# Attention of layer 1: row sums turned on the matrix engine and applied to the output, one operation for bias and maximum, turned blocks copied by two engines

## The reference

```
sc = (q . k) / sqrt(64) - slope * distance          # -inf for keys not chosen or in the future
pr = softmax(sc)                                     # exp(sc - max) / sum
o  = pr @ v
```

## Time and profile before

| | us |
|---|---|
| median of 3 runs | 1532.46 |
| lowest and highest | 1531.11, 1533.18 |
| the profiled execution | 1534.15 |
| its span, first to last instruction | 1532.3 |
| PE busy in the span | 1454.4 (95%) |
| DVE busy | 675.2 (44%) |
| ACT busy | 605.5 (40%) |
| POOL busy | 568.9 (37%) |

### The profile page before, as it was taken

The page is one execution under the profiler, slowest core; times in us unless marked ns, Lnnn a source line. Parts: engine busy times, 40 slices in busy tenths (PEclk is TensorE's granted clock), DMA queues, the critical chain, the costliest instruction groups (busy, mean ns, idle before and its releaser), DMA issues.

```text
span 1532.3 us, 24569 instructions
## 1 busy us (share of the span) xinstructions
PE 1454.4 (95%) x10321; PEld 1155.2 (75%) x10321; DVE 675.2 (44%) x1059; ACT 605.5 (40%) x872; POOL 568.9 (37%) x265
## 2 busy tenths in 40 slices
PE   7999989888899999999999999978999999999998
PEld 5787668888768888888887787744468888888886
DVE  4666656777563413223144207868823314132231
ACT  5525553434454313232233335557834313132231
POOL 3543331001033434434344242417944443434341
PEclk9999999999999999999999999998999999999999
DMA  4332200000113232322224121210012323232231
GB/s 141 97 96 69 79 5 3 3 3 3 58 58 107 83 110 83 110 82 97 95 82 106 60 83 55 83 55 1 1 56 84 109 88 105 83 102 89 89 102 55
DMA packets 128392, 110.00 MB, mean 72 GB/s; under 512 B 10678, under 2 KB 126512, under 8 KB 128304
## 3 DMA queue, kind: packets, MB, share of 16 engines
q1 hardware_dynamic: 127712, 107.64, 22.8%
q10 hardware_dynamic: 592, 1.07, 0.2%
HBM read 106.60 MB, written 2.10 MB: 71 GB/s over the span
## 4 chain that ended last, share of the span: by engine, by line
PE 78%; DVE 10%; ACT 5%; POOL 3%; issue 2%; DMA 1%; DVEq 0%; ACTq 0%; SPq 0%; POOLq 0%
PE ps L515 21%; PE ps L510 21%; PE ps L511 21%; PE ps L647 5%; DVE lower L1897 2%; DVE lower L1893 1%; POOL lower L2110 1%; PE ps L662 1%; ACT lower L1395 1%; PE ps L547 1%; POOL pw_lo L2001 1%; PE ps L655 1%; PE ps L624 1%; PE ps L751 1%; DVE lower L1676 1%
## 5 line engine op out<-in xcount | busy, mean ns | idle before, releaser
L2078 POOL TENSOR_TENSOR w_lo<-lower,w_hi 128x2048 fp32r<-128x2048 f32 x84 | 387.9, 4618 | 627.1 <-ACT w_hi L1051 627.1
L510 PE MATMUL ps<-h_hi,w_hi 128*128 128x512 f32 x792 | 314.5, 397 | 2.4 <-ACT h_hi L1056 1.7
L511 PE MATMUL ps<-h_hi,w_lo 128*128 128x512 f32 x792 | 313.1, 395 | 0.0
L1051 ACT ACTIVATE w_hi<-lower 128x2048 fp32r<-128x2048 f32 x84 | 160.2, 1907 | 242.8 <-PE ps L515 242.8
L515 PE MATMUL ps<-h_lo,w_hi 128*128 128x512 f32 x792 | 201.8, 396 | 0.4
L511 PE MATMUL ps<-a_hi,w_lo 128*128 128x512 f32 x480 | 189.1, 394 | 0.0
L510 PE MATMUL ps<-a_hi,w_hi 128*128 128x512 f32 x480 | 189.1, 394 | 0.0
L510 PEld LDWEIGHTS ps<-h_hi,w_hi 128*128 128x128 f32 x792 | 149.1, 188 | 41.6 <-issue 5.4
L515 PEld LDWEIGHTS ps<-h_lo,w_hi 128*128 128x128 f32 x792 | 148.7, 188 | 37.6 <-DVE h_lo L1599 2.0
L511 PEld LDWEIGHTS ps<-h_hi,w_lo 128*128 128x128 f32 x792 | 149.3, 188 | 35.3 <-issue 0.5
L1842 DVE TENSOR_TENSOR lower<-lower,ps 128x512 f32<-128x512 f32 x64 | 44.0, 688 | 268.7 <-PE ps L515 268.7
(11 more groups left out here) (358 smaller groups left out, 1991.0 us busy)
## 6 DMA issues: line engine op xcount, KB each, us to landing
lower<-in_mlp_w_dram SPq DMA_DIRECT2D x64, 1024.0 KB, 5.4
lower<-in_ev_w_in_dram SPq DMA_DIRECT2D x30, 512.0 KB, 3.8
lower<-in_od_w_in_dram SPq DMA_DIRECT2D x10, 1024.0 KB, 5.2
lower<-in_ev_w_out_dram SPq DMA_DIRECT2D x4, 1024.0 KB, 5.2
lower<-in_od_w_out_dram SPq DMA_DIRECT2D x4, 1024.0 KB, 5.1
out_dram<-lower SPq DMA_DIRECT2D x4, 512.0 KB, 3.2
lower<-in_od_w_in_dram SPq DMA_DIRECT2D x6, 256.0 KB, 3.8
upper<-in_x_dram SPq DMA_DIRECT2D x1, 1024.0 KB, 7.5
```

Source lines behind the costliest of these rows:

```text
L510: pe.matmul(o, wh, xh, start=(i_ == 0), stop=False)
L511: pe.matmul(o, wl, xh, start=False, stop=False)
L1051: act.activation(WH[:, u % 2, :, 0:w], RAW[:, u % 2, :, 0:w], ACT.Copy).then_inc(hi_ready, 1)
L2078: pool.tensor_tensor(WL[:, u % 2, :, 0:w], RAW[:, u % 2, :, 0:w], as_f32(WH[:, u % 2, :, 0:w]), ALU.subtract)\
```

## The change

The buffer isn't multiplied by the reciprocals any more. POOL spreads the two reciprocals of each row over 2 x 64 columns (`wide_sums`), PE turns this 128x128 block (`row_sums`) into bank 6, ACT copies the bank once for each block b (`sums_out`), and DVE multiplies the product of the values by it (`scaled_values`), while it moves it from bank 7 to SBUF. From there ACT makes the high part and POOL (instead of DVE) the rest.

Bias and row maximum are one operation (`tensor_tensor_reduce`), which needs the same factor for both inputs; so the queries are divided by the slope in advance (`QSCALE`, `QW`, four operations of 512 in place of one of 2048), the sign is turned, and the minimum is taken in place of the maximum.

The turned blocks of head 0 are still copied by ACT, and those of head 1 by DVE. PE's and DVE's loops get a new order, as the diff shows.

```diff
-        SLOPE = small(16)
-        QW = small(2)
+        QSCALE, QW = small(2 * PAIRS), small(2 * PAIRS)
...
+        PV = [L1[:, 20, :], flat(o_att + (2 * TT + 2) * W, W)]
+        RB = DIST
+        RSW = [flat(o_score + 4 * W + i * P, P) for i in range(3)]
...
+        at_pt = [sem("at_pt_act"), sem("at_pt_dve")]
+        VALUES, SUMS = 7, 6
+        def slope(b, p):
+            return float(np.float32(2.0) ** np.float32(-0.5 * (2 * (b % PAIRS * 2 + p) + b // PAIRS + 1)))
...
             def turned(n):
                 i, rows, wdt = rows_of(n)
                 for p in range(2):
-                    pe.wait_ge(at_n, 2 * n + p + 1)
+                    pe.wait_ge(at_p, 2 * n + p + 1)
                     if n >= 1:
-                        pe.wait_ge(at_pt, 2 * (n - 1) + p + 1)
+                        pe.wait_ge(at_pt[p], n)
...
             def values(b):
-                pe.wait_ge(at_pt, 2 * TT * (b + 1))
-                if b >= 2:
-                    pe.wait_ge(mix_lo, KT + b - 1)
+                if b >= 1:
+                    pe.wait_ge(at_pv, b)
+                for p in range(2):
+                    pe.wait_ge(at_pt[p], TT * (b + 1))
...
+            def row_sums(n):
+                i, rows, _ = rows_of(n)
+                pe.wait_ge(at_rw, n + 1)
+                if i == 0 and n >= TT:
+                    pe.wait_ge(at_rb, n // TT)
+                mm = pe.transpose(bank[SUMS][:, rows], RSW[n % 3], IDENT)
+                mm.then_inc(at_rs, 1)
 
             scores(0)
             scores(1)
...
                     scores(n + 2)
                 if n >= LAG:
                     turned(n - LAG)
+                    if n > LAG:
+                        row_sums(n - LAG - 1)
                     if n - LAG >= TT and (n - LAG) % TT == 0:
                         values((n - LAG) // TT - 1)
+            row_sums(STEPS - 1)
             values(2 * PAIRS - 1)
-            pe.wait_ge(mix_lo, KT + 2 * PAIRS - 1)
+            pe.wait_ge(at_rb, 2 * PAIRS)
...
-                    act.wait_ge(at_mx, 2 * n + p + 1)
+                    act.wait_ge(at_z, 2 * n + p + 1)
                     z = ZB[n % NZ][:, p, 0:wdt]
-                    act.activation(z, z, ACT.Exp, bias=NMX[:, col:col + 1],
+                    act.activation(z, z, ACT.Exp, bias=NMX[:, col:col + 1], scale=-1.0,
...
+            def sums_out(b):
+                act.wait_ge(at_rs, TT * (b + 1))
+                if b >= 1:
+                    act.wait_ge(at_pv, b)
+                act.activation(RB, bank[SUMS][:, :], ACT.Copy).then_inc(at_rb, 1)
...
             for n in range(STEPS + LAG):
                 if n < STEPS:
                     probs(n)
                 m = n - LAG
                 if m >= 0:
-                    if m >= TT + 1 and m % TT == 1:
+                    if m > TT and m % TT == 1:
+                        sums_out(m // TT - 1)
+                    if m > TT and m % TT == 3:
                         mixed(m // TT - 1)
                     out_turned(m)
...
-                dve.scalar_tensor_tensor(out=wide(L1[:, lo:lo + 4, :]), in0=wide(L1[:, lo:lo + 4, :]),
-                                         scalar=wgt, in1=wide(rs), op0=mul, op1=mul).then_inc(n_used, 1)
+                for c in range(4):
+                    x = L1[:, lo + c, :]
+                    ins = dve.scalar_tensor_tensor(out=x, in0=x, scalar=QW[:, lo + c:lo + c + 1] if lo < 8 else pc2(MKN),
+                                                   in1=rs[:, c, :], op0=mul, op1=mul)
+                ins.then_inc(n_used, 1)
...
+                dve.tensor_tensor_reduce(out=ZB[n % NZ][:, p, 0:wdt],
+                                         in0=BIAS[:, b // PAIRS, bias_off(i):bias_off(i) + wdt],
+                                         in1=bank[n % 2 * 2 + p][:, 0:wdt], scale=slope(b, p), scalar=3.0e38,
+                                         op0=add, op1=ALU.min, accum_out=NMX[:, col:col + 1]).then_inc(at_z, 1)
+
+            def out_turned(n):
                 i, rows, wdt = rows_of(n)
...
+                b = n // TT
+                dve.wait_ge(at_t, 2 * n + 2)
+                if i == 0 and b >= 2:
+                    dve.wait_ge(at_o, b - 1)
+                dve.tensor_copy(PT[b % 2][1][:, 0:i + 1, rows],
+                                bank[5][:, 0:wdt].rearrange("p (s t) -> p s t", t=P)).then_inc(at_pt[1], 1)
...
+            def scaled_values(b):
+                dve.wait_ge(at_rb, b + 1)
+                dve.wait_ge(at_o, b + 1)
+                if b >= 2:
+                    dve.wait_ge(mix_lo, KT + b - 1)
+                dve.tensor_tensor(PV[b % 2], bank[VALUES][:, :], RB, mul).then_inc(at_pv, 1)
+
+            for n in range(STEPS + LAG):
+                if n < STEPS:
+                    score(n, 0)
+                    score(n, 1)
+                if 1 <= n <= STEPS:
+                    inverse(n - 1)
                 m = n - LAG
-                if m >= TT + 1 and m % TT == 1:
-                    mixed_lo(m // TT - 1)
-            inverse(STEPS - 1)
-            mixed_lo(2 * PAIRS - 1)
+                if m >= 0:
+                    if m > TT and m % TT == 2:
+                        scaled_values(m // TT - 1)
+                    out_turned(m)
+            scaled_values(2 * PAIRS - 1)
...
+            def wide_sums(n):
+                col = n % 8 * 2
+                pool.wait_ge(at_ri, n + 1)
+                if n >= 3:
+                    pool.wait_ge(at_rs, n - 2)
+                pool.tensor_copy(RSW[n % 3].rearrange("p (q v) -> p q v", q=2),
+                                 RINV[:, col:col + 2].unsqueeze(2).broadcast_to([P, 2, HD])).then_inc(at_rw, 1)
+
+            def mixed_lo(b):
+                pool.wait_ge(mix_hi, KT + b + 1)
+                pool.tensor_tensor(HL[:, b, :], PV[b % 2], as_f32(HH[:, b, :]), ALU.subtract).then_inc(mix_lo, 1)
...
             for n in range(STEPS):
-                i, rows, wdt = rows_of(n)
-                pool.wait_ge(at_ri, n + 1)
-                for p in range(2):
-                    col = n % 8 * 2 + p
-                    z = ZB[n % NZ][:, p, 0:wdt]
-                    pool.tensor_scalar(z, z, RINV[:, col:col + 1], None, mul).then_inc(at_n, 1)
+                wide_sums(n)
+                if n >= 2 * TT and n % TT == 2:
+                    mixed_lo(n // TT - 2)
+            mixed_lo(2 * PAIRS - 2)
+            mixed_lo(2 * PAIRS - 1)
```

More of the change, by code:

```diff
@@ L1400, in out_turned @@
                 b = n // TT
-                for p in range(2):
[L1402 to L1407, removed]
+                act.wait_ge(at_t, 2 * n + 1)
+                if i == 0 and b >= 2:
+                    act.wait_ge(at_o, b - 1)
+                act.activation(PT[b % 2][0][:, 0:i + 1, rows],
+                               bank[4][:, 0:wdt].rearrange("p (s t) -> p s t", t=P),
+                               ACT.Copy).then_inc(at_pt[0], 1)
+            def sums_out(b):
[3 more added lines that the diff above has]
+                act.activation(RB, bank[SUMS][:, :], ACT.Copy).then_inc(at_rb, 1)
             def mixed(b):
-                act.wait_ge(at_o, b + 1)
-                act.activation(HH[:, b, :], bank[6 + b % 2][:, :], ACT.Copy).then_inc(mix_hi, 1)
+                act.wait_ge(at_pv, b + 1)
+                act.activation(HH[:, b, :], PV[b % 2], ACT.Copy).then_inc(mix_hi, 1)
             for n in range(STEPS + LAG):
@@ L1519, in _ @@
             dve.wait_ge(pads_zero, 1)
+            for i, col in enumerate((DQN, MQN)):
+                half = slice(i * PAIRS, (i + 1) * PAIRS)
+                dve.tensor_scalar(QW[:, half], QSCALE[:, half], pc2(col), None, mul)
             for c in range(4):
@@ L1952, in inverse @@
                 dve.wait_ge(at_p, 2 * n + 2)
+                if n >= 8:
+                    dve.wait_ge(at_rw, n - 7)
                 dve.reciprocal(RINV[:, cols], RSUM[:, cols]).then_inc(at_ri, 1)
[L1955 to L1961, removed]
-                score(n, 1)
-                top(n, 0)
-                if n >= 1:
+            def scaled_values(b):
[9 more added lines that the diff above has]
+                if 1 <= n <= STEPS:
                     inverse(n - 1)
-                top(n, 1)
                 m = n - LAG
-                if m >= TT + 1 and m % TT == 1:
-                    mixed_lo(m // TT - 1)
-            inverse(STEPS - 1)
-            mixed_lo(2 * PAIRS - 1)
+                if m >= 0:
[3 more added lines that the diff above has]
+            scaled_values(2 * PAIRS - 1)
             residual(1)
@@ L2026, in _ @@
             tile_lo(5)
-            for g in range(16):
-                col = (g % 2) * NH + g // 2
-                t.step(pool.memset(SLOPE[:, col:col + 1], -float(np.float32(2.0) ** np.float32(-0.5 * (g + 1)))))
+            for b in range(2 * PAIRS):
+                t.step(pool.memset(QSCALE[:, b:b + 1], -float(HD) ** -0.5 / slope(b, 0)))
+            t.settle()
```

(1 more changed line is left out.)

34 lines of the change are left out of this document (13 added, 21 removed).

## The result

The changed kernel takes 1555.4 us, the median of 4 runs between 1553.41 and 1556.06, and the kernel before 1531.78, also the median of 4 runs, the three of the table of before and one more. The ratio is 1.0155, with a 95% interval of 1.0139 to 1.0171: slower by 23.6 us. The profiled execution took 1556.06 us with a span of 1554.0, against 1534.15 and 1532.3 before. The attention stage, from its first scores to the first product of the projection, now runs from 1036.52 to 1142.06, which is 105.5 us, and ran from 1036.21 to 1120.32 before, 84.1 us. So it holds 21.4 of the 21.7 us of the span's difference.

What follows compares the result with a forecast made beforehand. A ring of waits between DVE and PE was taken to bound the changed kernel's attention stage. Terms 0.4 + 3.8 + 14.6 - 3.9 gave +14.9 us: 1547.4 against the median of 1532.46, range 1540 to 1556, 1538 to 1562 with the scan's case.

Steps and rivals of the forecast that it cites:

- the ring: Layer 1 attention: DVE score, PE scores, PE turned blocks, DVE copy take turns; 11.9 us a block against 9.46.
- j 0 to 1: From turned row block 0 to 1 (widths 128, 256): PE's sums, values, scores and turned blocks hide DVE's side; 3.61 us.
- j 1 to 2: From turned row block 1 to 2 (widths 256, 384): copy, fused operation, scores and turned blocks in turn; 2.55 us.
- j 2 to 3: From turned row block 2 to 3 (widths 384, 512): copy, first score, both heads' scores, eight turned blocks; 3.30 us.
- j 3 to 0: From turned row block 3 to 0 (widths 512, 128): copy, two DVE scores, one head's scores, turned blocks; 2.42 us.
- first turned step's end to first values: Early attention stage: 10.9 us at full clock, 15.3 with PE's terms doubled; middle 13.1 taken, +3.8 us.
- The scores' term: PE's pair of scores: 0.42, 0.63, 0.84, 1.06 us at widths 128 to 512; one head takes half.
- a rival of 8 in 100: PE's matrix clock falls to 1.2 GHz for half the attention stage: +25 us, 1572; 8 in 100.
- The scan's rate: Rival: DVE's fused operation runs at half rate, 0.133 us more per 128 elements: +10 us, 1557; 8 in 100.
- the sentence in the prediction: DVE's accumulator write as a second instruction, 0.08 us, four open in the ring: some 2 us more in the sum.
- The end of the stage: The ring opens as no scores(32) exists: 7.7 or 9.4 us, 8.6 taken against 12.5 before, -3.9 us.
- The faster rival: The ring doesn't bind; engines overlap and PE bounds the block at 8.5 us: 1522; 8 in 100.

Runs made afterwards that it cites:

- the later copy: Changed kernel with DVE copying the turned blocks of step n - 3, not n - 2, after score(n): 1522.83 us, ratio 0.9935 to the kernel before.
- The filled pauses: Changed kernel with PE turning the row-sum block five times instead of once in three steps of four: 1550.32 us, ratio 1.0105 to the kernel before.
- the kernel with the work behind the wait: Changed kernel plus one unused DVE maximum per step, between the wait for the turned blocks and the copy: 1564.19 us, ratio 1.0192 to the kernel before.

## Why the prediction was right, and where its sizes were off

The mechanism was right: the ring, its four steps, and which engine waits where. The four steps of the ring can be read off from copy to copy in DVE's rows: j 0 to 1 from 1082.98, where this copy begins as well, to 1086.61, 3.63 us (forecast 3.61); j 1 to 2, 2.64 (2.55); j 2 to 3, 3.48 (3.30); j 3 to 0, 2.58 (2.42). The sum is 12.33 against 11.9. The time lies within the range, 8 us above the forecast; as a difference, 14.9 us were forecast, and 21.7 lie between the two spans. The profile splits that:

| stretch | before | forecast | after |
|---|---|---|---|
| first turned step's end to first values | 9.3 | 13.1 | 14.9 |
| five blocks | 47.3 | 59.4 | 65.1 |
| last opening of the ring to the projection | 21.9 | 20.5 | 20.2 |

*The scores' term was too small.* I charged one head of a step with half the time of the pair. But the two heads' products, one on partitions 0 to 63 and one on 64 to 127, run side by side where neither waits, so the pair takes as long as one. The rows show the first two instructions of a pair of 512, one of each head: first the later copy, where PE doesn't wait, then the changed kernel.

```profile
1071.63 0.70 PE L972 MATMUL ps<-lower 64*128 64x512 f32 x2
```

```profile
1090.20 1.03 PE L972 MATMUL ps<-lower 64*128 64x512 f32 x2 [0.88 <-DVE lower L1975]
```

Together they take 0.70 us in the one and 1.03 in the other, where one alone takes 0.69. In the changed kernel each head waits for its own fused operation, and DVE ends the second 0.34 after the first (in DVE's rows it starts at 1090.06, and what follows it at 1090.40). So the pair takes 1.40 from start to start (1090.20 to 1091.60) in place of 1.06, and that of 384, behind operations of 128, takes 1.05 in place of 0.84: the pair's own time and one more fused operation. In j 3 to 0, where I had the second operation in the sum, the head behind it takes the pair's 0.42 and not 0.21. The row of 384 in the earlier trace rows, 1.17 behind a wait, had it in sight; I had struck it out as "contains a wait". Together this is some 0.76 us in a block. Against it, the fused operations in the ring are 0.05 cheaper each than L1937, 0.2 in all, and from the first turned block to the copy it is up to 0.13 less than I had. What is left is the 0.45 of 12.33 less 11.88. Over five blocks the ring's price is 5 x 0.45 = 2.2 of the 5.7 us missed in them.

*The clock had no term in the middle of the stage.* I had it as a rival of 8 in 100 with the half of the stage slow, and at the ends as "the middle" of two values. It was neither. Ahead of the first values the granted clock was mostly half (0.67 from 1040 to 1050, 0.50 from 1046 to 1054), and the stretch took 1.8 us more than forecast. Of these, 0.4 are a slip of mine: the ring with PE's terms doubled is 16.1 and not 15.3, so the middle is 13.5. The other 1.4 are clock and ring together, which the rows don't part. Behind the first values, two short spells make the most of 65.1 - 5 x 12.33 = 3.4 us. The filled pauses confirm the sign and about the size: the stage is 5.2 us shorter, 2.2 ahead of the first values and 3.0 behind them (the spans differ by 6.0, but 0.7 of it lies ahead of the stage). By the Trainium skill ("TensorE: Matmul & The Clock Gate", "Part 1: The HAM clock gate") activity releases the throttle. This experiment agrees: with more work in the pauses, the clock is 1.00 from 1056 on where it was 0.91 from 1060 to 1100. But the kernel with the work behind the wait keeps 1.00 with longer pauses, so more than the pauses decides.

*The fused operation.* The scan's rate didn't come: it takes 0.68 at 512, a little less than L1937's 0.74. The rule of the Trainium skill that an accumulated result is a second instruction ("VectorE: DVE Perf Modes", "Two Vector instructions with no wait between them") holds in the trace, as DVE_READ_ACCUMULATOR2_ANT of 0.08 us; but its price is nothing, as the next fused operation starts with it (both at 1090.06). By the sentence in the prediction it would have been 2 us.

*The end of the stage* was about as forecast, the opened ring 20.2 against 20.5. In part that is luck: I had taken the middle between the two clocks for the last values, and they ran at the full one, for which my sum was 19.6. The last multiplication, split and rest are hidden by the projection, as forecast, since its first product starts at 1142.06, right behind the last values. Ahead of the stage the four operations of 512 took 2.74 in place of 2.35, as forecast. POOL was idler than I had it, 4.22 of 20 us and not a third, as its spread takes 0.29 us and not 0.61; it was off the path either way.

*The faster rival* was right about work and wrong about order. With the order changed its 8.5 us are nearly reached: 8.77 and 8.63.

What stays open is why the granted clock falls in one block and not in another of the same pattern, and why it doesn't fall in the kernel with the longest pauses. So a forecast can give the clock's part of such a stage only as a range.

## What to carry to other kernels

When work moves from one engine's queue to another's, draw the circle of who waits for whom between two engines within one step, and sum it with the hand-overs: each engine's sum of work says nothing if the circle is longer. A circle can be opened without moving any work to another engine, by a new order in the queue of either one; here that was worth some 32 us, and turned a loss of 24 us into a gain of 8. Where two operations release two products that could run side by side, the second operation's time stands in the circle as well. An instruction's price is that of its side of the wait: 1.38 us a block on one side, 0 on the other.

## What the runs showed of the hardware

- Two products of 64 rows each, one on partitions 0 to 63 and one on 64 to 127, run side by side: the first instructions of a pair of 512 take 0.70 us together and 0.69 alone. When the second has to wait 0.34 us longer for DVE than the first, the pair takes 1.40 in place of 1.06.
- `scalar_tensor_tensor` of 128x384 with one input in PSUM takes 0.61 us with its factor in an SBUF column and 0.55 with it in the instruction; two of them take 1.13 and 1.01.
- Added PE work in pauses shortened the kernel by 0.5% (ratio 1.0155 to 1.0105): no spell at the half clock was left behind the first values. Longer pauses in another kernel (13.70 us a block in place of 12.33) went with the full clock from 1062 on.
- POOL's spread of two columns to 128x128 took 0.29 us, where I had 0.61 from a 128x128 multiplication.
